# Opening of a two-layer diffusion block: order of the first transfers, the first tile and the value weights

## The reference

```python
c_act = silu(c); c_ctx_act = silu(c_ctx)
for l in range(2):
    mod = c_act @ w_ada[l] + b_ada[l]              # shift, scale, gate, twice
    h  = layer_norm(x)  * (1 + sc_a)  + sh_a       # latent tokens
    hc = layer_norm(xc) * (1 + scc_a) + shc_a      # context tokens
    u  = [hc; h] @ w_in[l] + b_in[l]               # q/kv latents, f, nq, nk, nv, gates
    ...  # latent attention, 2-D Fourier mixing, neighbourhood attention with table rpb
    x = layer_norm(alpha * x + g_a * y)
    ...  # 32 experts, two per token; layer_norm
```

## Time and profile before

| what | us |
|---|---|
| median of 3 runs | 2732.73 |
| lowest and highest | 2728.9, 2738.07 |
| the profiled execution: its own time | 2731.71 |
| its span, from the first to the last instruction | 2729.8 |
| PE busy | 2477.0 (91%) |
| DVE busy | 927.2 (34%) |
| ACT busy | 626.2 (23%) |
| DMA engines, mean rate | 221 GB/s |
| mean granted TensorE clock, share of 2.4 GHz | 0.966 |

### The profile page before, as it was taken

The page is one execution under the profiler, slowest core; times in us unless marked ns, Lnnn a source line. Parts: engine busy times, 40 slices in busy tenths (PEclk is TensorE's granted clock), DMA queues, the critical chain, the costliest instruction groups (busy, mean ns, idle before and its releaser), DMA issues.

```text
span 2729.8 us, 32976 instructions
## 1 busy us (share of the span) xinstructions
PE 2477.0 (91%) x12749; PEld 1531.6 (56%) x12749; DVE 927.2 (34%) x1764; ACT 626.2 (23%) x1174; POOL 346.5 (13%) x409
## 2 busy tenths in 40 slices
PE   5999899999999889989985999999999888989984
PEld 3768556788885533434332768567887433434331
DVE  3335466622224720000004534556332720000003
ACT  2221345622220111101102421446331011111100
POOL 1241000001111220000002520000011220000001
PEclk8999999999999889999998999999999989999997
DMA  9571001322217589999996560004433789999994
GB/s 279 206 250 47 6 1 13 78 68 61 70 43 235 222 352 420 421 421 417 420 421 240 199 207 27 7 1 87 97 101 124 295 354 419 421 420 405 420 420 162
DMA packets 238331, 604.39 MB, mean 221 GB/s; under 512 B 67328, under 2 KB 143504, under 8 KB 188640
## 3 DMA queue, kind: packets, MB, share of 16 engines
q1 hardware_dynamic: 210786, 528.65, 51.6%
q0 software_dynamic: 24512, 63.13, 6.6%
q10 hardware_dynamic: 2880, 10.49, 1.0%
HBM read 585.70 MB, written 38.16 MB: 229 GB/s over the span
## 4 chain that ended last, share of the span: by engine, by line
PE 67%; DMA 15%; DVE 10%; ACT 3%; SPq 3%; issue 2%; POOL 0%; DVEq 0%; ACTq 0%; POOLq 0%
PE slot L1127 20%; PE abank L708 18%; PE vbank L708 10%; DMA arena<-in_w_down_e 6%; DMA arena<-in_w_up_e 6%; PE slot L1028 3%; PE vbank L904 2%; SPq L2682 2%; DMA arena<-in_w_in 1%; DVE nmx L1542 1%; DVE stat L1262 1%; PE abank L791 1%; PE slot L931 1%; PE vbank L851 1%; PE vbank L700 1%
## 5 line engine op out<-in xcount | busy, mean ns | idle before, releaser
L1127 PE MATMUL slot<-arena 128*64 128x512 f32 (+2 forms) x3264 | 825.8, 615 | 86.0 <-DMA arena<-in_w_up_e 61.8
L1127 PEld LDWEIGHTS slot<-arena 128*64 128x64 f32 (+2 forms) x3264 | 296.7, 146 | 562.1 <-issue 553.8
L708 PE MATMUL abank<-round,round 128*128 128x512 f32 (+1 forms) x1792 | 491.3, 355 | 8.1 <-DVE round L1359 3.6
L708 PEld LDWEIGHTS abank<-round,round 128*128 128x128 f32 x1792 | 317.9, 189 | 71.5 <-issue 14.8
L1894 DVE TENSOR_TENSOR arena<-slot,arena 128x512 f32<-128x512 f32 x76 | 52.5, 691 | 801.0 <-ACT arena L2215 507.9
L708 PE MATMUL abank<-hT_low,round 128*128 128x512 f32 (+1 forms) x896 | 317.6, 354 | 0.0
L708 PE MATMUL vbank<-round,round 128*128 128x512 f32 (+2 forms) x1312 | 306.1, 359 | 3.1 <-issue 2.0
L708 PEld LDWEIGHTS vbank<-round,round 128*128 128x128 f32 x1312 | 226.3, 189 | 38.2 <-issue 4.5
L708 PEld LDWEIGHTS abank<-hT_low,round 128*128 128x128 f32 x896 | 168.6, 188 | 23.7 <-issue 0.5
L1634 DVE TENSOR_TENSOR arena<-vbank,arena 128x512 f32<-128x512 f32 x72 | 43.4, 602 | 304.5 <-PE vbank L708 304.2
L1028 PE MATMUL slot<-arena 128*128 128x512 f32 x320 | 140.1, 599 | 3.4 <-POOL arena L2378 3.4
(11 more groups left out here) (299 smaller groups left out, 2699.8 us busy)
## 6 DMA issues: line engine op xcount, KB each, us to landing
arena<-in_w_gate_e SPq DMA_DIRECT2D x128, 1024.0 KB, 27.1
arena<-in_w_up_e SPq DMA_DIRECT2D x128, 1024.0 KB, 27.2
arena<-in_w_down_e SPq DMA_DIRECT2D x128, 1024.0 KB, 28.1
arena<-in_w_ada POOLq DMA_DIRECT2D x80, 512.0 KB, 4.9
arena<-in_w_in SPq DMA_DIRECT2D x48, 512.0 KB, 4.2
arena<-in_w_in SPq DMA_DIRECT2D x8, 2048.0 KB, 14.8
h_rows<-arena ACTq DMA_DIRECT2D x20, 512.0 KB, 6.6
arena<-y_rows SPq DMA_DIRECT2D x20, 512.0 KB, 8.4
```

Source lines behind the costliest of these rows:

```text
L708: last = pe.matmul(to, x, y, start=(k == 0 and q == 0), stop=(k == len(terms) - 1 and q == 2))
L1127: last = pe.matmul(to[at, cols], x[:, at], w[:, at_w, :], start=first, stop=final)
```

## The change

The diff does these things:

1. The position tables move to the end of the constants, are loaded after the weights of `f` with `tokid` and the table `rpb`, and are waited for later (`mla_in`, `NLATER`). The first transfer of constants is 979 columns in place of 2515.
2. The conditioning vectors come as 8 rows of 128 each into the buffer of the biases, and are turned with them by PE; ACT and DVE read them from PSUM. DVE scales the table `rpb` after the last `tile_lower`, not before the first.
3. PE turns tile 0 before the last `summed`, and ACT scales tile 0 before it rounds the value weights.
4. DVE forms the lower half of tile 0 first, then the value weights' lower half in two pieces with the statistics of tile 2 between them, and PE waits for the second piece in the middle of a value product.
5. The latent rows come in 32 transfers of 16 rows. Each has a fixed column j, and writes the partitions j, j+8, j+16 and so on. The second load in the middle of the layer uses the same function.
6. PE makes 4 + 2 + 2 + 2 + 3 + 4 products with `keep_clock`.

```diff
-NCONST = 4
+NLATER = 2
...
+        def grid_rows(ap, t, j):
+            return ap[0].rearrange("(r t b j) d -> t j b r d", r=ROWS, b=2, j=BCOL)[t - CTX_TILES, j]
...
+                    keep_clock(slot[1], 4)
                     for j in range(MOD_FIRST):
+                        if j:
+                            summed(j - 1)
+                            keep_clock(slot[1], 2)
                         pe.wait_ge(first_in[j], 16)
...
-                        if j:
-                            summed(j - 1)
+                    z_turned(0, 0)
                     close(summed(MOD_FIRST - 1), mod_groups)
+                    keep_clock(slot[1], 3)
...
+                        if L == 0 and t == 1:
+                            keep_clock(slot[1], 4)
+                            chunk()
...
                 for k, (wh, wl, xh, xl) in enumerate(terms):
+                    if upper_half and k == len(terms) // 2:
+                        pe.wait_ge(w_lower, upper_half)
...
                 if L == 0:
-                    value_lower()
                     tile_lower(0)
-                    dve.wait_ge(x_in[1], 32)
-                    moments(x_sb[:, 2, :], 2, mv).then_inc(stats_ready, 1)
+                    value_lower(0)
                     for t in range(2, NTILES):
-                        if t + 1 < NTILES:
-                            dve.wait_ge(x_in[t], 32)
-                            moments(x_sb[:, t + 1, :], t + 1, mv).then_inc(stats_ready, 1)
+                        dve.wait_ge(x_in[t - 1], 128)
+                        moments(x_sb[:, t, :], t, mv).then_inc(stats_ready, 1)
+                        if t == 2:
+                            value_lower(1)
+                        tile_lower(t - 1)
                         centred(t)
-                        tile_lower(t - 1)
                         nv_taken(t - 2)
                     tile_lower(NTILES - 1)
+                    table_scaled(0)
...
-            def load_x():
-                for b in range(GRID_W // BCOL):
-                    sp.dma_start(x_sb[64 * (b % 2):64 * (b % 2) + 64, CTX_TILES + b // 2, :], grid_block(a["x"], b)
-                                 ).then_inc(x_in[1 + b // 2], 16)
+            def load_x(lo, hi):
+                for t in range(lo, hi):
+                    for j in range(BCOL):
+                        sp.dma_start(x_sb[j:P:BCOL, t, :], grid_rows(a["x"], t, j)).then_inc(x_in[t - 1], 16)
```

More of the change, by code:

```diff
@@ L652, in input_biases @@
             def input_biases(L):
-                pe.wait_ge(ada_in, 48 + 16 * L)
+                n = 40 if L else 40 + 2 * KD
+                pe.wait_ge(ada_in, 80 + 16 * L)
                 ps = vec()
-                last = pe.transpose(ps[:, 0:40], bin_rows[0:40, :], ident[0:40, 0:40])
+                last = pe.transpose(ps[:, 0:n], bin_rows[0:n, :], ident[0:n, 0:n])
                 close(last, vgroups)
@@ L718, in by_token @@
                     (hT_hi[:, k, t * P:(t + 1) * P], low_tiles[:, t, k, :], w_hi[:, k, :], wl[:, k, 0:cols])
-                    for k in range(KD)]), vgroups)
+                    for k in range(KD)], part_of(L, name, m) + 1 if m else None), vgroups)
             def by_column(name, w_hi, blocks, hooked, between=None):
@@ L737, in by_column, with z_turned @@
                 chunk_end()
-            pe.wait_ge(consts_in, 16 * NCONST)
+            def z_turned(L, t):
+                pe.wait_ge(z_ready, ZB(L, "h1") + t + 1)
+                for half in range(2):
+                    ps = act()
+                    for q in range(4):
+                        k = 4 * half + q
+                        last = pe.transpose(ps[:, q * P:(q + 1) * P], z2[t % 2][:, k * P:(k + 1) * P], ident)
+                    close(last, agroups)
+                    mark["z_used", L, t, half] = st["g"]
+            pe.wait_ge(consts_in, 16)
             input_biases(0)
@@ L743, in _ @@
                 qt, qb = qtiles(L), qblocks(L)
-                if L == 0:
-                    chunk()
                 for t in range(NTILES + 1):
                     if t < NTILES:
[L749 to L756, removed]
+                        if L or t:
+                            z_turned(L, t)
+                        if L == 0 and t == 1:
+                            keep_clock(slot[1], 4)
+                            chunk()
                         if L and t == 0:
@@ L1299, in mod_chunk, with table_scaled @@
                 dve.tensor_tensor(mod_sb[:, cols], ps[:, :], mod_sb[:, cols], ALU.add).then_inc(vec_taken, 1)
+            def table_scaled(L):
+                dve.wait_ge(rpb_in, 32 * (L + 1))
+                dve.tensor_scalar(rpb_z[0:HEADS * 15, 0:RP], rpb_z[0:HEADS * 15, 0:RP], 1.0 / NAT_SCALE, None,
+                                  ALU.mult).then_inc(bias_ready, 1)
             def mod_end(L):
@@ L1946, in take @@
                 return abank[n % 2]
-            act.wait_ge(consts_in, 16 * NCONST)
-            act.activation(csT[:, :, :], crow[:, :, :], ACT.Sigmoid).then_inc(sig_ready, 1)
+            act.wait_ge(consts_in, 16)
+            act.wait_ge(groups_done, vgroups[0])
+            act.activation(csT[:, :, :], vbank[0][:, 40:56].rearrange("p (v k) -> p k v", v=2), ACT.Sigmoid
+                           ).then_inc(sig_ready, 1)
             for L in range(DEPTH):
@@ L1983, in _ @@
                 else:
+                    value_upper()
                     act.wait_ge(vec_taken, mark["modT", L])
@@ L1998, in _ @@
                     act.copy(hT_hi[:, :, t * P:(t + 1) * P], h_row[t % 2]).then_inc(hT_split[0], 1)
+                    if L == 0 and t == 0:
+                        value_upper()
                     if L and t + 1 < NTILES:
@@ L2489, in _, with load_table @@
             w_in, b_in = a["w_in"], a["b_in"]
[L2490 to L2494, removed]
+            sp.dma_start(cst[:, 0:C_COS], cst_d[:, 0:C_COS]).then_inc(consts_in, 16)
+            def load_table(L):
+                with nc.allow_non_contiguous_dma("two copies of the position table"):
+                    table = a["rpb"][L].rearrange("h r c -> (h r) c")
+                    sp.dma_start(rpb_z[0:HEADS * 15, 15:31], table[:, 7:23]).then_inc(rpb_in, 16)
+                    sp.dma_start(rpb_z[0:HEADS * 15, 47:78], table).then_inc(rpb_in, 16)
             def mod_loads(L):
@@ L2503, in mod_loads @@
                              ).then_inc(ada_in, 16)
[L2504 to L2507, removed]
+                if L:
+                    load_table(L)
             def mod_rest(L):
```

66 lines of the change are left out of this document (34 added, 32 removed).

## The result

| what | before | after |
|---|---|---|
| median, us | 2731.67 (5 runs) | 2746.19 (5 runs) |
| lowest and highest | 2728.9, 2738.07 | 2742.43, 2748.94 |
| the profiled execution: its own time | 2731.71 | 2742.43 |
| its span | 2729.8 | 2740.6 |
| mean granted TensorE clock | 0.966 | 0.967 |

The changed kernel is slower: ratio 1.0052, 95% interval 1.004 to 1.0063, 14.5 us between the medians. The two profiled executions lie 10.7 us apart, since the one after is the lowest of its five.

The account below looks back on a forecast made before the run. The prediction took the DMA stream as the bound before 42.6 us, then PE until `f` at 90.0. Slow latent landings, sharing and clock losses put `f` at 104.0, 14.0 later: 2731.7 + 14.0 = 2745.7, written 2746, range 2735 to 2775.

Parts of the forecast that it names:

- case A: The forecast: two engines carry the latent transfers at 24.5 GB/s each, the stream before them faster; 2746 us, chance 0.55.
- Start of the stream: Opening: tables and two element-wise loads leave the head, whole stream 3.1 us earlier, first chunk issued at about 4.65.
- First tile and weights: Opening: `modT` at 36.1 against 42.2 before; first value product could start at 44.4 instead of 51.55.
- Two engines at full rate: Latent transfers: views begin with 2 and 16, so two engines at 24.5 GB/s each, a tile in 10.7 us.
- Case C: Latent transfers: two engines at 14.4 GB/s, tile 5 landing at 115.8; 2778 us, chance 0.15.
- Tiles: Latent rows in the opening: tiles 2, 3, 4 and 5 land at 47.7, 58.4, 69.8 and 85.8.
- Sharing with POOL's quarters: Opening: POOL's four quarters put 131 KB on each of the two engines while tile 5 moves, 5.3 us later.
- From landing to `f`: After tile 5 lands: statistics, POOL, centring, turning, two tiles' products, 15.8 us; plus 1.5 and 0.9 for the clock.
- `f` at 104.0: Start of the Fourier product, where the value products end: 104.0 against 90.0 before, 14.0 us later.
- Case D: Opening: two engines, but no sharing with POOL's quarters (-5.3) and the clock held (-2.4); 2738 us, chance 0.12.
- Case B: Latent rows spread over 8 or 16 engines, each later step 7.4 us earlier; 2724.3 us, chance 0.10.
- break-even mark: Opening: tile 5's landing decides slower or not; 74.2 us is break-even.

Follow-up runs that it names:

- e7: Kernel before with only the tables moved last and the conditioning vectors turned by PE, value weights rounded behind the wait for `modT`: 2729.74 us, ratio 0.999.
- e6: Changed kernel, its 32 latent transfers kept, without the 17 `keep_clock` products: 2742.43 us, ratio 1.004.
- e1: Changed kernel with the latent rows again in 8 transfers of 64 rows, both loads: 2730.47 us, ratio 0.9994.
- e5: e4 with the order of the latent transfers' source view turned, 8 columns by 8 grid rows: 2727.89 us, ratio 0.9988.
- e3: Changed kernel with POOL's first quarters of the next chunk issued after the sixth deviation, not before it: 2743.73 us, ratio 1.0046.
- e4: Changed kernel with the old 8 latent transfers of 64 rows and without the 17 `keep_clock` products: 2726.31 us, ratio 0.9981.

## Why the prediction was right

The forecast was case A, 2746; the median is 2746.19. The mechanism was right, two engines for the latent rows; one term, the sharing, was too large. Step by step, predicted and then measured:

- **Start of the stream**: 3.1 us earlier, first chunk at 4.65. Measured 3.45 earlier, 4.32. e7 puts its worth at 2.9 to 3.7 us of `f`.
- **First tile and weights**: `modT` 36.1, first product 44.4. Measured 35.08 and 43.59; the last chunk's products took the 1.92 at the higher clock that was chosen for them, and e6 shows that it is the clock products that gave it. The value weights landed at 38.4, not 37.0, still ahead of ACT, which wanted them at 39.3. Slips in this part changed nothing: 10 clock products lie ahead of the last chunk, not 11, the steps listed up to `modT` add up to 4.3 us, not 4.5, and 42.0 and 2.25 make 44.25, not 44.4.
- **Two engines at full rate**, the step on which all hung: predicted a share of 0.12 to 0.15 at some 50 GB/s, measured 0.13 at 52. e1 shows it is the whole loss, e5 that the order of the source view made the old transfers slow. Case C (14.4 GB/s) falls by both. One row behind the inference was not as clean as it was read: between 85.5 and 88.5 POOL's queue moved 0.15 of the 0.62 MB, beside the writes of `rpb_rep`.
- **Tiles** at 47.7, 58.4, 69.8, 85.8: DVE starts on tiles 2, 4 and 5 at 46.4, 67.6, 81.5. The first two are early by 1.3 and 2.2. The last is early by 4.3.
- **Sharing with POOL's quarters**, the term that was mis-sized: 5.3 taken. From tile 2 to tile 4 it is 21.2 us with the bias between, 10.2 a tile; from tile 4 to tile 5 it is 13.9, so 3.7 more. e3, which moves the quarters away, has tile 5 there 2.7 us earlier, and still 11.15 us between tiles 4 and 5. So the quarters cost 2.7; the other 1.0 stands without them, and its cause is open. The Trainium skill ("DMA: Bandwidth & Descriptors", section "Queues, rings and completion order") has engines take turns between queues; the trace agrees that tile 5 is held up, but by half of the full 5.3: three of the four quarters landed behind it.
- **From landing to `f`**: 18.2 predicted with the clock's losses, 19.2 measured. The products took 12.99, 1.8 over the 11.16 at full clock: from 80 to 90 PE was busy for only 4.25 us and the granted clock was 0.74, from 90 to 100 it was 0.92.
- **`f` at 104.0** predicted, 100.71 in the profile. So is the profiled execution, 2742.43 where the sum gave 2745.7. That the median meets the 2746 is luck in this part: the profiled execution was the fastest of five, 3.8 us under their median, and the sum had no term for that.
- **Second load**: predicted as hidden. Between 845 and 960 us DVE does not wait for it, and the span grew by no more than `f` moved (10.8 and 10.7).
- **Weights of `f`** behind the latent rows: hidden; PE goes on from the last value product at 100.71 without a wait.

Case D was 2738, for no sharing and the clock held. The runs lie above it, and e3, which takes the sharing away and has 11.80 for the last products, still has 2743.73. But half of its condition on the sharing was met (2.7 of 5.3), so the profiled `f` lies between the 104.0 of A and the 96.3 that D makes of it. Case B, the spread over more engines, was priced too high: e1, which has eight engines, reached `f` 5.9 us earlier, not 7.4, because ACT and DVE then set a tile (6.77 us), and its median is only 1.4 us under that of the kernel before. The break-even mark, tile 5 at 74.2, was passed by 7.3 us.

## What to carry to other kernels

Before a transfer is cut to touch more partitions, look at the first dimension of both views: it sets the number of engines, and a view that begins with 2 put 2 MB on two engines. A slow transfer may be slow because its engines read at one large distance at the same time; turning the order of the source dimensions raised 133 to 201 GB/s, if the receiver can live with the order. And what keeps the clock up has to be weighed at the end of the kernel: here it saved 1.7 us of one chunk's products ahead of a wait for a transfer, 1.1 us at `f` with fast transfers (e1 against e4), and that kernel was 4.2 us slower in the end.

## What the runs showed of the hardware that was not expected

- Transfers on few engines hold their issuer: the second 16 transfers of 64 KB kept SP for 19.72 us, 1.2 us each, about the time in which two engines move 64 KB at 52 GB/s. So the weights of `f`, which use all 16 engines, were issued at 63.44, and at 33.59 in e4. In the old form the eight took 5.74.
- While old latent transfers and the weights of `f` move together, all engines count as busy and move little. In e4, from 39 to 41 us:

```profile
39.00:41.00 2.00, 1.77 (x8) 1.25 (x8) 0.00 (x0) 1.97 (x5) 0.00 (x0) 0.50 1.04 153
```

That is 153 GB/s at a share of 1.04, against 390 at 1.05 in the stream of the chunks.

- Two engines that served two queues finished tile 5 2.7 us later (81.49 against 78.80) for 131 KB each of the other queue, less than the 5.3 that one engine needs for it alone.
